# Query heads turned in pairs, their high and low parts split over the two row halves, and full high and low key sets

## The reference

```python
proj = rmsnorm(x, norm_g) @ w_in            # rq rk rv rg | aq ak av ag | iq ik iw
# retention branch: 4 heads of 128, rotated q and k, chunk-causal with decay, a state
# attention branch: 8 query heads of 64 on 2 key heads, 8 indexer heads of 64 on one key
aq, ak, iq, ik = rope(first 16 of 64 dims)
logits = relu(einsum('bqhd,bld->bqhl', iq, ik))
index  = einsum('bqhl,bqh->bql', logits, iw)      # masked by 64-row chunks
sel    = top_k(index, min(256, n_keys // 4))
p      = softmax over the selected keys of (aq . ak) * 64 ** -0.5
ao     = p @ av
y      = rmsnorm(x + concat(ret * silu(rg), ao * silu(ag)) @ w_out)
```

## Time and profile before

| | us |
|---|---|
| median of 3 runs (lowest, highest) | 974.39 (972.59, 982.64) |
| span of the profiled execution | 971.1 |
| PE busy | 873.8 (90%) |
| DVE busy | 546.9 (56%) |
| ACT busy | 355.3 (37%) |
| POOL busy | 189.9 (20%) |

### The profile page before, as it was taken

The page is one execution under the profiler, slowest core; times in us unless marked ns, Lnnn a source line. Parts: engine busy times, 40 slices in busy tenths (PEclk is TensorE's granted clock), DMA queues, the critical chain, the costliest instruction groups (busy, mean ns, idle before and its releaser), DMA issues.

```text
span 971.1 us, 13082 instructions
## 1 busy us (share of the span) xinstructions
PE 873.8 (90%) x4413; PEld 709.0 (73%) x4413; DVE 546.9 (56%) x1337; ACT 355.3 (37%) x786; POOL 189.9 (20%) x374
## 2 busy tenths in 40 slices
PE   4789989989989999699898999999997999999983
PEld 3677767777767768567686778888876888888872
DVE  5433677696686867667532564544465644444422
ACT  5545464656364565546340121211124311111110
POOL 0333413222204031111002132222212011111100
PEclk9899998999999999869759899999997999999997
DMA  9210110102010000101224221111235432222121
GB/s 278 67 30 19 29 56 7 55 8 55 8 45 14 16 22 5 33 1 55 66 65 146 71 55 38 49 56 41 70 96 174 132 87 86 86 86 86 65 65 54
DMA packets 28273, 60.16 MB, mean 62 GB/s; under 512 B 7152, under 2 KB 9600, under 8 KB 28224
## 3 DMA queue, kind: packets, MB, share of 16 engines
q1 hardware_dynamic: 21920, 40.19, 15.1%
q0 software_dynamic: 6304, 19.36, 5.9%
HBM read 48.44 MB, written 11.09 MB: 61 GB/s over the span
## 4 chain that ended last, share of the span: by engine, by line
PE 62%; DVE 15%; issue 9%; ACT 5%; POOL 4%; DMA 3%; SPq 1%; DVEq 0%; POOLq 0%; ACTq 0%
PE bank L777 40%; PE bank L898 5%; PE bank L881 3%; PE bank L887 3%; PE bank L880 3%; DVE work L1413 1%; DVE top L1411 1%; DVE probs L1474 1%; PE bank L839 1%; PE bank L763 1%; DVE w_lo L1282 1%; PE bank L840 1%; DVE xT_lo L1317 1%; DMA stage<-in_w_out 1%; ACT pT L1117 1%
## 5 line engine op out<-in xcount | busy, mean ns | idle before, releaser
L777 PE MATMUL bank<-w_hi,xT_hi 128*128 128x512 f32 (+1 forms) x576 | 232.4, 403 | 13.9 <-DVE xT_lo L1317 9.6
L777 PE MATMUL bank<-w_lo,xT_hi 128*128 128x512 f32 (+1 forms) x576 | 226.2, 393 | 0.0
L777 PE MATMUL bank<-w_hi,xT_lo 128*128 128x512 f32 (+1 forms) x576 | 225.8, 392 | 0.0
L777 PEld LDWEIGHTS bank<-w_hi,xT_hi 128*128 128x128 f32 x576 | 111.9, 194 | 41.0 <-issue 12.7
L777 PEld LDWEIGHTS bank<-w_hi,xT_lo 128*128 128x128 f32 x576 | 111.6, 194 | 21.7
L777 PEld LDWEIGHTS bank<-w_lo,xT_hi 128*128 128x128 f32 x576 | 111.9, 194 | 19.6
L898 PE MATMUL bank<-v_sb,pT 128*128 128x64 f32 x648 | 98.7, 296 | 8.5 <-ACT pT L1117 8.0
L898 PEld LDWEIGHTS bank<-v_sb,pT 128*128 128x128 f32 x648 | 92.5, 216 | 15.4 <-ACT pT L1117 14.1
L1359 DVE SCALAR_TENSOR_TENSOR idx<-bank,iw_s,idx 128x384 f32<-128x384 f32 (+5 forms) x93 | 53.2, 610 | 41.5 <-ACT bank L1152 40.7
L1117 ACT COPY pT<-bank 128x512 f32<-128x512 f32 (+3 forms) x104 | 49.6, 494 | 66.1 <-PE bank L887 65.6
L887 PE MATMUL bank<-ident,probs 128*128 128x128 f32 x324 | 62.1, 309 | 9.5 <-ACT probs L1106 9.4
(11 more groups left out here) (186 smaller groups left out, 1386.8 us busy)
## 6 DMA issues: line engine op xcount, KB each, us to landing
xin<-in_x_prompt SPq DMA_DIRECT2D x48, 256.0 KB, 3.9
stage<-in_w_in SPq DMA_DIRECT2D x40, 256.0 KB, 2.7
early<-in_w_in SPq DMA_DIRECT2D x4, 1024.0 KB, 6.4
y_row<-in_x_prompt SPq DMA_DIRECT2D x16, 256.0 KB, 4.7
stage<-in_w_out SPq DMA_DIRECT2D x16, 256.0 KB, 3.4
out<-y_row POOLq DMA_DIRECT2D x8, 512.0 KB, 2.9
retained<-ro POOLq DMA_DIRECT2D x9, 256.0 KB, 2.4
mixed<-retained POOLq DMA_DIRECT2D x9, 256.0 KB, 3.1
```

The source lines that it names most:

```text
L777: mm = pe.matmul(out, (lo if which == 2 else hi)[:, k, :], (w_lo if which == 1 else w_hi)[slot][:, k, 0:width], start=(i == 0), stop=(i == ...
```

## The change

Each projected head is kept once. Four turned blocks hold two heads each: head 2j in rows 0 to 63, head 2j + 1 in rows 64 to 127. ScalarE writes each head's high part into its own row half, VectorE the low part into the other half (it reads one row half and writes the other). So an even head is [high; low], an odd one [low; high], for attention as for the indexer. Keys are kept as two full sets, `kT_hi` and `kT_lo`, both halves alike, and a score is two 128-row matmuls. Cached keys are turned as they come, without the doubling by GpSimd, and ScalarE and VectorE write them to both halves (4 + 4 instructions for `ci`, 8 + 8 for `ck`, of 64 rows each). `ck` comes in one transfer into `xin` on a semaphore of its own. The scratch output of the x squares moves from `aq_row` to `probs[1]` (with a wait on VectorE at head 1), v is stored from `v_sb`, and the scratch of the rotation lies in unused columns of two weight slots. Cut to its core:

```diff
-        kT = sb("kT", [P, KVH, NK], F32R)
+        kT_hi, kT_lo = (sb(f"kT_{x}", [P, KVH, NK], F32R) for x in ("hi", "lo"))
-        q_row = sb("q_row", [P, AH, 2, HD])
-        aq_row = sb("aq_row", [P, AH, 2, HD])
+        q_row = sb("q_row", [P, AH, HD])
+        aq_row = sb("aq_row", [P, AH, HD])
+        rope_a, rope_b = (w[:, :, KVW:KVW + ROT] for w in spare)
...
-            take(("turn_iq0", "A", t))
-            take(("turn_iq1", "A", t))
+            take(("turn_iq", "A", t))
...
-            take(("turn_aq0", "A", t))
-            take(("turn_aq1", "A", t))
+            take(("turn_aq", "A", t))
...
+        def half_rows(a):
+            return slice(a * HD, (a + 1) * HD)
+        def packed(t, dst, a, r):
+            if t != SAMPLE:
+                return dst[r].rearrange("p (j a) n -> p j a n", a=2)[:, :, a, :]
+            return dst[r, 0:AH // 2, a * DEC:(a + 1) * DEC]
...
-                for i in {4: (27, 28), 5: (29, 30), 6: (31,), 7: (32, 33, 34)}.get(t, ()):
+                for i in {4: (27, 28), 5: (29, 30), 6: (31,), 7: (32,)}.get(t, ()):
...
+                if i == item_no["rk", STAGES]:
+                    wait_filled(sp, ("x1", "R", 0))
+                    sp.dma_start(xin[:].rearrange("p (b n) -> p b n", n=P), kc).then_inc(ck_in, 16)
...
             def turn_queries(name, t, row):
+                turn_rows((name, "A", t), row[:].rearrange("p h d -> p (h d)"), AH // 2)
...
-                        pe.matmul(out, aqT_hi[:, h, :], kT[:, kv, a:b], start=True, stop=False)
-                        pe.matmul(out, aqT_lo[r, h % (heads_of(t) // KVH), :], kT[r, kv, a:b], start=False, stop=True)\
-                          .then_inc(*fills(key))
+                        pe.matmul(out, aqT[:, h, :], kT_hi[:, kv, a:b], start=True, stop=False)
+                        pe.matmul(out, aqT[:, h, :], kT_lo[:, kv, a:b], start=False, stop=True).then_inc(*fills(key))
...
             def square_x(t):
-                if t >= 2:
-                    wait_filled(act, ("turn_aq1", "A", t - 2))
-                act.activation(aq_row[:].rearrange("p h a d -> p (h a d)"), xin[:], ACT.Square,
-                               accum_out=x_sq[:, 0:1]).then_inc(x_squared, 1)
+                act.activation(probs[1][:, 0:D], xin[:], ACT.Square, accum_out=x_sq[:, 0:1]).then_inc(x_squared, 1)
...
             def hi_queries(name, t, dst):
+                key = (name, "A", t)
+                for a in range(2):
+                    hi(key, packed(t, dst, a, half_rows(a)), turned_heads(t, key, a))
...
+            def hi_cached_keys(half):
+                key = ("turn_ck", half)
+                wait_filled(act, key)
+                for g in range(KVH):
+                    for to in range(2):
+                        ins = act.copy(kT_hi[half_rows(to), g, half * BW:(half + 1) * BW], of(key)[half_rows(g), :])
+                ins.then_inc(hi_ready, 1)
...
-                    twice(q_row[:], of(key)[:], AH).then_inc(*drains(key))
+                    act.copy(q_row[:].rearrange("p h d -> p (h d)"), of(key)[:]).then_inc(*drains(key))
...
-                    act.copy(vw_row[:], of(key)[:, 3 * HD:KVW]).then_inc(rowed, 1)
+                    act.copy(iw_row[:], of(key)[:, 5 * HD:KVW]).then_inc(rowed, 1)
...
+            def lo_queries(name, t, dst):
+                key = (name, "A", t)
+                for a in range(2):
+                    dve.wait_ge(hi_ready, hi_no(f"{name}{a}", "A", t))
+                    ins = dve.tensor_tensor(packed(t, dst, a, half_rows(1 - a)), turned_heads(t, key, a),
+                                            packed(t, dst, a, half_rows(a)).bitcast(F32), ALU.subtract)
+                ins.then_inc(*drains(key))
...
+            def lo_cached_keys(half):
+                dve.wait_ge(hi_ready, hi_no(f"ck{half}", "A", SAMPLE))
+                for g in range(KVH):
+                    for to in range(2):
+                        ins = dve.tensor_tensor(kT_lo[half_rows(to), g, s], of(key)[half_rows(g), :],
+                                                kT_hi[half_rows(g), g, s].bitcast(F32), ALU.subtract)
+                ins.then_inc(*drains(key))
...
-                    for g in range(KVH):
-                        ins = lo_key(g, s, of(key)[:, (1 + g) * P:(1 + g) * P + n])
-                    ins.then_inc(*drains(key))
+                    dve.tensor_tensor(kT_lo[:, :, s], of(key)[:, P:3 * P].rearrange("p (g n) -> p g n", n=P)[:, :, 0:n],
+                                      kT_hi[:, :, s].bitcast(F32), ALU.subtract).then_inc(*drains(key))
...
+                    if h == 1:
+                        dve.wait_ge(x_squared, min(t + 2, TILES))
...
-                rotate(aq_row[:], 2 * AH, t).then_inc(q_roped, 1)
+                rotate(aq_row[:], AH, t).then_inc(q_roped, 1)
...
+                wait_drained(pool, ("kv", "A", t))
...
-                    double("ck", 0, q_row, ("turn_ci", 1))
```

More of the change, by code:

```diff
@@ L451, in hybrid_stream_step @@
                 take_rows(1)
[L452 to L454 removed]
+            take(("turn_aq", "A", t))
+            for name, banks in (("turn_ci", t == NT - 1), ("turn_ck", 2 * (t == SAMPLE))):
                 for b in range(banks):
@@ L508, in hybrid_stream_step @@
             if t == NT - 1:
-                hi_order += [("ci0", t), ("ci1", t)]
+                hi_order += [("ci", t)]
             if t == SAMPLE:
-                hi_order += [(f"ck{b}", t) for b in range(4)]
+                hi_order += [(f"ck{b}", t) for b in range(2)]
         hi_at = {(s, *x_of(t)): i + 1 for i, (s, t) in enumerate(hi_order)}
@@ L862, in attend @@
             def attend(t):
-                for half in range(2):
-                    wait_drained(pe, (f"turn_aq{half}", "A", t))
+                wait_drained(pe, ("turn_aq", "A", t))
                 if t == SAMPLE:
-                    for b in range(4):
+                    for b in range(2):
                         wait_drained(pe, ("turn_ck", b))
@@ L1068, in between @@
                     if t:
-                        wait_filled(act, ("turn_aq1", "A", t - 1))
-                    twice(aq_row[:], of(key)[:], AH).then_inc(*drains(key))
+                        wait_filled(act, ("turn_aq", "A", t - 1))
+                    act.copy(aq_row[:].rearrange("p h d -> p (h d)"), of(key)[:]).then_inc(*drains(key))
                 elif name == "iq":
@@ L1175, in _ @@
                 if t == NT - 1:
+                    hi_cached_indexer()
+                if t == SAMPLE:
                     for half in range(2):
-                        hi(("turn_ci", half), kiT_hi[:, half * BW:(half + 1) * BW])
-                if t == SAMPLE:
-                    for b in range(4):
-                        hi(("turn_ck", b), kT[:, b % KVH, b // KVH * BW:(b // KVH + 1) * BW])
+                        hi_cached_keys(half)
                 if 2 <= t <= 5:
@@ L1441, in between @@
                 elif name == "turn":
-                    for half in range(2):
-                        lo_below(t, (f"turn_iq{half}", "A", t), half)
+                    lo_queries("turn_iq", t, iqT)
                     key = ("turn_kv", "A", t)
@@ L1518, in _ @@
                     choose(0)
-                for g in range(KVH):
-                    r = slice(HD * g, HD * g + HD)
-                    key = (f"turn_aq{g}", "A", t)
-                    lo(key, hi_no(*key), packed(t, aqT_lo, 0, r), packed(t, aqT_hi, g, r), turned_heads(t, key, r))
+                lo_queries("turn_aq", t, aqT)
                 if t == NT - 1:
+                    lo_cached_indexer()
+                if t == SAMPLE:
                     for half in range(2):
-                        s = slice(half * BW, (half + 1) * BW)
-                        lo(("turn_ci", half), hi_no(f"ci{half}", "A", t), kiT_lo[:, s], kiT_hi[:, s])
-                if t == SAMPLE:
-                    for b in range(4):
-                        key = ("turn_ck", b)
-                        dve.wait_ge(hi_ready, hi_no(f"ck{b}", "A", t))
-                        lo_key(b % KVH, slice(b // KVH * BW, (b // KVH + 1) * BW), of(key)).then_inc(*drains(key))
+                        lo_cached_keys(half)
                 if 2 <= t <= 5:
@@ L1794, in guess_threshold @@
                 pool.tensor_tensor(above, above, mean, ALU.add).then_inc(guessed, 1)
-            def double(what, half, row, free):
-                i = item_no[what, half]
-                pool.wait_ge(*staged[i])
-                wait_filled(pool, free)
-                pool.tensor_copy(row[:], raw(i)[:].rearrange("p (b d) -> p b d", d=HD).unsqueeze(2)
-                                 .broadcast_to([P, AH, 2, HD])).then_inc(doubled, 1)
             def store_attended(t):
```

109 lines of the change are left out of this document (51 added, 58 removed).

## The result

The changed kernel takes 934.73 us, median of 4 runs (932.81 to 935.3); the kernel before took 973.89 in the same session (972.59 to 982.64, 4 runs). The ratio is 0.9583, 95% interval [0.9542, 0.9624]: 39 us less. Run again beside three of the experiments, the changed kernel gave 936.41 (0.9646 [0.9601, 0.9692]).

The account below looks back on a forecast made before the run. TensorE was taken as the bound (90% busy, 62% of the chain), changing with VectorE within phase A's tiles. Terms -27.0 - 1.5 + 2.8 + 2.0 = -23.7 us take span 971.1 to 947.4; plus 3.3, 950.7, stated 950, range 936 to 963.

Parts of the forecast that it names:

- The gap is the row form: Score matmuls alternate 128 and 64 rows; all at 128, each loses 0.19 us, 0.30 at half clock: 44.6 us of TensorE.
- The rival that it is something else of the score: Score matmuls: the gap comes from operands or banks and stays; 974 us, chance 0.06.
- Tiles 4 to 6, VectorE becomes the bound: VectorE's waits of 15.7 us for the second score matmul shrink to 1.7: 14.0 us gained.
- The turned blocks, ScalarE, GpSimd: Half the turned blocks, shorter ScalarE copies and half GpSimd's rotation: costed at nothing beyond tile 0's 1.5 us.
- The rival of 957 us: VectorE pays 0.3 us an instruction for reading one row half and writing the other: +7 us, 957, chance 0.10.
- `ck`: Cached keys ahead of tile 8: VectorE's four conversion instructions become eight, 2.84 us becomes 5.7: +2.8 us.
- `ci`: Cached indexer keys: tile 8's index starts 2.5 us later, covered by ScalarE's 3.37 us wait for the x scale: nothing.
- The clock: Falls at the ends of tiles 4 to 6 cost +2 us in all; tile 8 stays at half clock.
- one of my own signs of being wrong: The list of what would show the prediction wrong, including a granted clock that differs in phase A.
- my first rival: Tile 8: the clock comes back after the first twelve scores, some 22 us instead of 32; 940 us, chance 0.25.
- Tile 7: Matmuls at half clock for heads 2 and 3 give 2.4 us, the next head 0.8: 3.2 us gained.
- The slower rival: Tiles 4 to 6: the clock falls and stays down, +15 us a tile; one tile 965, three 995; chance 0.04.

Follow-up runs that it names:

- rows128_in_old: The kernel before with only the second score matmul changed, to all 128 rows: 936.66 us, ratio 0.9632.
- rows64_in_new: The changed kernel with its second score matmul on 64 rows again, in all tiles: 967.22 us, ratio 0.9962.
- blocks_turned_twice: The changed kernel with each set of four query blocks turned twice into the same bank, 72 more turns: 935.30 us, ratio 0.9633.
- warm_and_rows64_tile_8: The changed kernel with tile 8's second score matmuls on 64 rows and 44 extra matmuls ahead of that tile: 942.87 us, ratio 0.9736.
- rows64_both_products: The changed kernel with both matmuls of every score on 64 rows, leaving out the queries' low parts in the first: 955.77 us, ratio 0.9806.

## Why the prediction was right, and why its size was wrong

- The gap is the row form. Right, and so was its size: from 0.37 to 0.18 us at full clock, from 0.62 to 0.32 at half. The rival that it is something else of the score falls with rows128_in_old.
- Tiles 4 to 6, VectorE becomes the bound. Right: forecast 12.5 with the keys and the clock, measured 13.3; VectorE's waits went from 15.7 to 3.5 us (1.7 were forecast) and nothing took their place. Tiles 0 to 3: 4.2 and 4.8.
- The turned blocks, ScalarE, GpSimd: nothing, right (rows64_in_new, blocks_turned_twice). Keys in one instruction: 0.41 for 0.42 us.
- Crossing the row halves: nothing, right. VectorE's L1334 takes 0.69 us for 64 rows and 512 columns, as it did when it read and wrote the same half (0.69). The rival of 957 us falls.
- `ck`: +3.0 for +2.8. `ci`: its cover held with 0.89 us left.
- The clock: wrong, and this is the step that failed. I sized tile 8 as 24 x 0.30 us less at an unchanged half clock, 6.3, and put +2 on the sum for falls elsewhere. The attention of tile 8 became 13.9 us shorter, of which 12.7 are what the clock was worth in warm_and_rows64_tile_8. That the granted clock would differ in phase A was one of my own signs of being wrong, and it came. A clock that comes back in tile 8 was my first rival, with a chance of 0.25 and 940 us. I set it low because 38.20 us of turned blocks and values without a pause hadn't brought the clock back. That row could not bear this: the tile had mixed-form scores at its start and between its heads, so it said nothing of how the tile goes without them. The reason that I gave for the rival, drains in the score stretches, isn't borne out either: rows64_both_products has no such gaps within a head and stays at half clock, warm_and_rows64_tile_8 has them and its profile stays at full.
- Tile 7: forecast 3.4 with the clock as it was, 9.4 measured, and the clock again is the difference: 17 us at half clock before, some 3 after, around the first scores. The rival priced tile 8 alone, and at 10 us of gain over the forecast where 7.2 were measured; that its 940 less tile 7's 6.0 us make 934 is in part luck.
- The slower rival, clock lost in tiles 4 to 6: the clock dips behind the ends of these tiles, but the stages are 13.3 us shorter all the same.

## What to carry to other kernels

Look for matmuls of 64 rows between matmuls of 128: where the forms alternated, each product came 0.19 us later at full clock and 0.30 at half, and filling up the rows with a product that isn't needed cost nothing that a run shows. Where a stretch runs at half clock and the change alters what TensorE does right at its start, give both levels of the clock as results with nearly equal chances: here the level was worth 12.7 us, and the gaps themselves 1.4 or somewhat more. A row that shows a clock staying down speaks only of the kernel that it was taken from.

## What wasn't expected of the hardware

- With gaps in it, TensorE's work kept a clock that was up (1.00 from 452 to 480 us in the profile of warm_and_rows64_tile_8, 1.00 for 40 us of tile 7 in rows64_in_new), yet in tile 8 the same scores didn't raise a fallen one (0.50 for 39 us).
- 64-row scores without a gap between them didn't raise it in tile 8 either (0.50 to the tile's end), where twelve full-row scores of the same columns did.
- A fall in tile 7 lasted 17 us with the old scores and 3 to 7 us with full rows; it came with either.
- 2.78 us of idling behind 44 matmuls at full clock were followed by scores at half clock.
